# Decoder trunk, last stage of the experts: down chunks multiplied by output half, half of the result evicted ahead, read-back rows added at another place

## What is computed

```python
logits = jnp.dot(t, w_router); top_logit, top_idx = lax.top_k(logits, 2)
top_w = jax.nn.softmax(top_logit, axis=-1)
gate = jnp.einsum('tk,tke->te', top_w, jax.nn.one_hot(top_idx, 8))
for e in range(8):
    out = out + gate[:, e:e + 1] * swiglu(t, w_gate[e], w_up[e], w_down[e])   # 1024 -> 3584 -> 1024
h = h + out
u = rmsnorm(h, ple_norm_gain[i])
h = h + (p[i] @ w_ple[i]) * jax.nn.sigmoid(u @ w_ple_gate[i])
return rmsnorm(h, final_norm_gain)
```

## Time and profile before

| | us |
|---|---|
| three runs | 1537.55, 1538.18 (median), 1538.69 |
| profiled execution: its time | 1538.69 |
| its span in the trace | 1536.9 |
| what lies outside the span | 1.8 |

### The profile page before, as it was taken

How to read it: one execution, slowest core, us unless ns; L and a number is a source line. 1 busy time by engine, 2 the same in 40 slices (tenths; PEclk the granted TensorE clock), 3 DMA queues, 4 the chain that set the end, 5 groups by cost and what they waited for, 6 DMA issues and landing times.

```text
span 1536.9 us, 21230 instructions
## 1 busy us (share of the span) xinstructions
PE 1515.6 (99%) x7976; PEld 1278.5 (83%) x7976; DVE 1230.9 (80%) x1100; ACT 995.1 (65%) x852; POOL 56.7 (4%) x76
## 2 busy tenths in 40 slices
PE   7999999999999999999999999999999999999998
PEld 6988888888998888888888888888888888888876
DVE  5776545557686689888889889988988889898897
ACT  6544444346725367787786787687677787777666
POOL 5000000000000000000000000000000000010000
PEclk9999999999999999999999999999999999999999
DMA  9432765555533589999999999999999999999990
GB/s 300 142 111 84 256 207 186 186 168 182 165 113 121 172 292 363 379 376 382 379 374 384 381 370 387 373 373 389 371 376 387 372 374 393 367 381 387 372 390 30
DMA packets 206787, 453.38 MB, mean 295 GB/s; under 512 B 12488, under 2 KB 31504, under 8 KB 206480
## 3 DMA queue, kind: packets, MB, share of 16 engines
q1 hardware_dynamic: 200368, 439.22, 79.2%
q0 software_dynamic: 2880, 10.49, 1.8%
q10 hardware_dynamic: 3488, 2.99, 0.7%
HBM read 444.80 MB, written 7.86 MB: 295 GB/s over the span
## 4 chain that ended last, share of the span: by engine, by line
PE 95%; DVE 3%; ACT 1%; DMA 0%; issue 0%; SPq 0%; DVEq 0%; ACTq 0%
PE bank L1607 29%; PE bank L1609 28%; PE bank L1608 28%; PE bank L2106 2%; PE bank L1698 2%; DVE wlo L953 1%; PE bank L1805 1%; PE bank L1758 1%; PE bank L1602 1%; DMA raw<-in_w_in_dram 0%; PE bank L1772 0%; PE bank L2079 0%; PE bank L1707 0%; PE bank L1732 0%; PE bank L2088 0%; PE bank L1747 0%
## 5 line engine op out<-in xcount | busy, mean ns | idle before, releaser
L953 DVE TENSOR_TENSOR wlo<-raw,whi 128x2048 fp32r<-128x2048 f32 x415 | 936.4, 2288 | 143.1 <-ACT whi L604 91.7
L604 ACT ACTIVATE whi<-raw 128x2048 fp32r<-128x2048 f32 x341 | 636.6, 1911 | 34.3 <-DMA raw<-in_w_exp_down_dram 17.8
L1607 PE MATMUL bank<-whi,uTh 128*128 128x512 f32 (+1 forms) x1304 | 512.0, 393 | 0.9 <-DVE uTl L1019 0.5
L1609 PE MATMUL bank<-whi,uTl 128*128 128x512 f32 (+1 forms) x1304 | 503.8, 386 | 0.0
L1608 PE MATMUL bank<-wlo,uTh 128*128 128x512 f32 (+1 forms) x1304 | 502.8, 386 | 0.0
L1609 PEld LDWEIGHTS bank<-whi,uTl 128*128 128x128 f32 x1304 | 245.0, 188 | 50.7
L1607 PEld LDWEIGHTS bank<-whi,uTh 128*128 128x128 f32 x1304 | 245.2, 188 | 49.0 <-DVE uTl L1019 0.7
L1608 PEld LDWEIGHTS bank<-wlo,uTh 128*128 128x128 f32 x1304 | 245.4, 188 | 46.6
L1607 PE MATMUL bank<-whi,hTr 128*128 128x512 f32 x528 | 207.2, 392 | 0.4 <-DVE hTr L1506 0.4
L1609 PE MATMUL bank<-whi,hTr 128*128 128x512 f32 x528 | 205.7, 390 | 0.0
L1608 PE MATMUL bank<-wlo,hTr 128*128 128x512 f32 x528 | 205.5, 389 | 0.0
(11 more groups left out here) (294 smaller groups left out, 1084.1 us busy)
## 6 DMA issues: line engine op xcount, KB each, us to landing
raw<-in_w_exp_gate_dram SPq DMA_DIRECT2D x112, 1024.0 KB, 5.6
raw<-in_w_exp_up_dram SPq DMA_DIRECT2D x112, 1024.0 KB, 6.2
raw<-in_w_exp_down_dram SPq DMA_DIRECT2D x112, 1024.0 KB, 5.7
raw<-in_w_in_dram SPq DMA_DIRECT2D x28, 1024.0 KB, 5.5
raw<-in_w_ffn_gate_dram SPq DMA_DIRECT2D x11, 1024.0 KB, 5.1
raw<-in_w_ffn_up_dram SPq DMA_DIRECT2D x11, 1024.0 KB, 5.2
raw<-in_w_ffn_down_dram SPq DMA_DIRECT2D x11, 1024.0 KB, 4.9
raw<-in_w_out_dram SPq DMA_DIRECT2D x8, 1024.0 KB, 5.3
```

Source lines behind the costliest of these rows:

```text
L604: nc.scalar.activation(whi[:, s % SPLIT, :], raw[:, s % RAW, :], ACT.Copy).then_inc(hi_a, 1)
L953: return V.tensor_tensor(wlo[:, n % RAW, :], raw[:, n % RAW, :], whi[:, n % SPLIT, :].bitcast(F32), ALU.subtract).then_inc(lo_ready, 1)
L1607: T.matmul(o, sth, mvh, start=start, stop=False)
L1609: return T.matmul(o, stl, mvh, start=False, stop=stop)
```

## The change

Three edits. (1) In a down chunk PE goes over the halves outside and the rows of weights inside: banks 5, 5, 6, 6; in the last chunk of an item it counts a new semaphore `first_half` when bank 5 is finished. (2) ACT's `y_out` waits for `first_half` ahead of the first half's copy, and for the whole last chunk only ahead of the second's. (3) In the last item DVE calls `add_experts(0)` and `add_experts(1)` behind its work for chunks 38 and 39, ahead of `last_slots` and no longer behind it. The semaphores `fgp0` and `fgp1` become one that counts to two.

```diff
-        fgp = sems("fgp", DEPTH)
+        fgp = sem("fgp")
...
-                dve.wait_ge(fgp[l], 1)
+                dve.wait_ge(fgp, l + 1)
...
             def y_out(i):
-                act.wait_ge(consumed, i * EXP_LOADS + (NSTATIC + EXP_LOADS))
                 act.wait_ge(scattered, i * 16 + 16)
                 for q in range(2):
+                    if q == 0:
+                        act.wait_ge(first_half, i + 1)
+                    else:
+                        act.wait_ge(consumed, i * EXP_LOADS + (NSTATIC + EXP_LOADS))
                     nc.scalar.activation(ysb[:, q * NC:(q + 1) * NC], bank(5 + q), ACT.Copy).then_inc(y_ready, 1)
...
-            item(last_item, EXP_LOADS + 1)
+            def other_rows(n):
+
+                if LAST_UP + 1 <= n <= LAST_UP + TT:
+                    add_experts(n - LAST_UP - 1)
+
+            item(last_item, EXP_LOADS + 1, other_rows)
             last_slots()
-            add_experts(0)
-            add_experts(1)
             add_last(0)
             add_last(1)
...
-                        for c, q in [(c, q) for c in range(2) for q in range(2)]:
+                        for q, c in [(q, c) for q in range(2) for c in range(2)]:
                             cc = 2 * hf + c
                             s = slice(q * NC, (q + 1) * NC)
                             last = product(bank(5 + q), exhT[r % 2][0][:, cc, :], exhT[r % 2][1][:, cc, :], wh[:, c, s], wl[:, c, s],
                                            start=r == 0 and cc == 0, stop=end and c == 1)
+                            if end and q == 0 and c == 1:
+                                last.then_inc(first_half, 1)
```

More of the change, by code:

```diff
@@ L314, in trunk @@
         slot_ready, last_y = sem("slot_ready"), sem("last_y")
+        first_half = sem("first_half")
         consumed = sem("consumed")
@@ L1676, in forget @@
                     if c0 + n == SEQ:
-                        last.then_inc(fgp[l], 1)
+                        last.then_inc(fgp, 1)
                 def step(s):
```

## The result

The changed kernel takes 1541.22 us (median of 11 runs, 1539.47 to 1544.83); the kernel before took 1538.53 us in the same comparison (11 runs, 1536.91 to 1540.55). The ratio is 1.0019, 95% interval 1.0011 to 1.0028; the medians are 2.7 us apart, the changed kernel slower.

A forecast was written before the change was run, and what follows sets the result against it. PE was taken to bound the items and last stage, with DVE's add_last and ACT's square setting the stretch between. Banks 0, copies 0 and DVE order +1.84 us on 1538.18 gave 1540.0 us, range 1538.3 to 1541.5.

The forecast's parts named there:

- Bank order, and copies in the items: Down chunks and y_out of items 0 to 6: nothing gained or lost; bank order bounded at 1.1 us either way.
- Copies in the last item: y_out of the last item: first copy 1.36 us earlier, but DVE not free until 1498.05; alone worth about 0.2 us.
- `add_experts` ahead of `last_slots`: DVE behind chunk 42's low part: last_slots ends at 1498.13, PE's products and the end come 1.84 us later.
- the hand-over: From DVE's selectors to PE's products: PE's wait for slot_ready might cost 0.3 us more, upper bound 2.1 us.
- The rival by the clock: PE's clock falls in the 2.6 us gap before the products: about +3.1, together +4.9 us, median 1543.1; chance 0.09.
- PE's slack of 0.26 us: PE's wait ahead of tile 0's transposes, taken off the clock rival's 3.4 us of lost work.
- the likeliest case: Whole kernel: banks 0, copies 0, DVE order +1.84 us, giving a median of 1540.0 us.
- the range: Median time of the changed kernel: 1538.3 to 1541.5 us.
- its own sign of being wrong: Behind the gap ahead of the selector products: PE's clock row showing less than 1.00 would prove the prediction wrong.
- The last stage: Behind tile 0's transposes, from 1504 on: PE is full, so the end moves by the same 1.84 us.

The follow-up runs named there:

- e1: The changed kernel with the third edit undone (bank order and early copy stay): 1539.26 us for 1539.07 us of the kernel before, ratio 1.0000.
- f1: The changed kernel itself, timed and profiled again, on another chip: 1542.32 us for 1539.20 us of the kernel before, ratio 1.0017.
- g2: One more profiled execution of the unaltered changed kernel; no median given; its selector products took 3.69 us.
- e2: The kernel before with the third edit alone (old bank order, old y_out): 1541.22 us for 1539.07 us of the kernel before, ratio 1.0020.
- e3: The changed kernel with last_slots between add_experts(0) and add_experts(1): 1538.82 us for 1539.07 us of the kernel before, ratio 0.9996.
- f2: The changed kernel with 20 unread transposes on PE ahead of its wait for slot_ready: 1539.78 us for 1539.20 us of the kernel before, ratio 1.0003.
- g3: The changed kernel with 20 unread transposes ahead of PE's wait for slot_ready, timed again: 1541.06 us for 1539.17 us of the kernel before, ratio 1.0013.

## Why the prediction was right, point by point

- **Bank order, and copies in the items.** Nothing, as forecast: in `e1` both edits stand and the ratio is 1.0000. The waits that PE had in the items of the changed kernel's first profile (0.9 us from 650 to 1490) come and go: the executions `f1` and `g2` of the same kernel have none there, and `e2`, without the two edits, has 0.3.
- **Copies in the last item.** I put 0.2 us on the early copy alone. It measured 0.01 (7.85 for 7.86 us). The products did come earlier, by 0.92 us, but DVE's fourth addition was not what bound. The prediction has DVE ending last and ACT's square earlier; yet the chain of the kernel before runs from the second addition over the square, and in `e1` DVE waits 0.17 us for ACT behind all four additions. A term that was too big by its whole size, with no effect on the sum, since the third edit covered it.
- **`add_experts` ahead of `last_slots`.** Forecast +1.84 us; in the trace +1.90, and +1.88 in `e2` alone. The steps: additions from 1492.19, forecast 1492.07; selectors done at 1498.26, forecast 1498.13; both differ by the 0.1 us by which that execution was late. From the selectors' end to PE's products it took 0.24 us and not 0.06: the hand-over that no row showed, for which the upper bound had allowed 0.3. So the products came 2.04 us later and not 1.84. The transposes came only 1.90 us later, because DVE no longer waited for ACT ahead of its reciprocal: this started 0.67 us behind the start of the fourth addition (1502.90 for 1502.23) and 0.79 us before (1500.88 for 1500.09). ACT's square came 1.76 us later, counted from the last down matmul, where I had 1.3 to 1.5. `e3` shows the condition: it costs only what the selectors come later than PE.
- **The rival by the clock** had a chance of 0.09 and was taken to happen or not. It does both: 1 in 4 profiled executions, +3.1 us foretold and 3.0 measured (12.78 less 9.76), +4.9 in all foretold and 4.92 measured. That the price fits so well is in part luck. The clock was low for 6.8 us in `f1` too, 3.4 us of lost work, but 0.4 us of it were lost in the gap, where nothing ran, and PE's slack of 0.26 us, which I took off, saves nothing, since DVE's additions wait for the same products and the norm comes later with them. The rows were also misread: 1.08 us is PE's longest wait in the routing stage, not in the trace. At the kernel's start PE waits 2.87 us for DVE, and the eight transposes behind that took 1.97 us, where those at 1503.06 took 1.09; this was a hint of slower matmuls behind a wait, though with no dense work ahead of it. A fall in some executions fits the timed median (+2.7, again +3.1), which lies above the trace's 1.9, and the comparison with the filled gap, at +1.2 us, speaks for it; how often it happens is not shown. The step that failed is the one that took this as one case among others and the likeliest case as the median; a fall in some executions belongs into the forecast's own range. How many timed runs have it can't be told: a timed run gives one mean clock for the whole run, in steps of 0.001 or 1.5 us, and the falls of the routing stage (below) lower it as much as one in the gap. The rule of the Trainium skill ("TensorE: Matmul & The Clock Gate", "Why this matters for your kernels"), that idle gaps between bursts bring the clock back to its lower level, agrees with the gap of 4.2 us here. The gap of 2.8 us is shorter than those that the rule warns of, so that by its letter it did not foretell this rival; the fall came there all the same, in one execution of five.
- **The number.** The median of 1541.22 lies inside the range, 0.3 us below its upper edge and 1.2 above the likeliest case: 0.35 us because the kernel before measured 1538.53 and not 1538.18, 0.06 us by the trace, and 0.8 us that the trace of the profiled execution doesn't show. `f1`, the same kernel once more, has 1542.32, outside it (the kernel before was 0.7 us higher in that set, too). And its own sign of being wrong, a clock below 1.00 behind the gap, is there in one execution of four. The mechanism was right; that the median stayed in the range owes something to luck.
- **The last stage** takes up nothing, as forecast: PE is busy in 25.00 of 25.00 us behind the transposes.

## What to carry to other kernels

Work that is moved ahead on one engine pushes something back on the same engine: look at what stands between the old and the new place, and who waits for it. Here there was no gap to fill, only three short operations that another engine waited for; the right move was to take those out of the full stretch, to any place behind their inputs where the engine has time. A result that is ready earlier (the copy here) is worth what the last of its partners allows, so find the partner before speeding up the first. And a wait of PE can cost more than its length: filling it with transposes that nobody needs gave back most of the surplus where the wait itself could not be removed. It is no sure cure: the kernel fills the waits of its routing stage with such transposes already, and the clock falls there in every profiled execution.

## What the runs showed of the hardware

PE's clock behind a gap is not a property of the kernel alone. With 2.8 us of idle PE behind 840 us of dense matmuls the same program kept 1.00 in three profiled executions and went to 0.50 in one; with 4.2 us it went to 0.50 in the one execution that was profiled, and in none of the three profiled ones with the gap filled. The longer gap was not the dearer one: the fall cost 3.0 us behind 2.8 us of gap and 1.7 us behind 4.2. In the first the clock was down before the products began (0.50 over 1497.5 to 1498), in the second it fell about 1 us after they had begun (0.70 over 1502 to 1504).

The clock also falls in the routing stage, in all 14 profiled executions here (0.50 to 0.63 over 532 to 536), although PE is busy there and the kernel already puts filling transposes into its waits. From PE's transposes at about 525 us to those of the second item's tokens at about 650 it took 126.1 us in one execution and 122.8 in another. The first of the two is `f2`, with these stretches in it (clock 0.83, 0.50, 0.52):

```profile
525.00:532.00 7.00, 5.19 (x35) 4.79 (x34) 4.79 (x20) 2.26 (x2) 0.53 (x1) 0.83 0.90 297
532.00:536.00 4.00, 4.00 (x22) 4.00 (x21) 1.53 (x10) 1.35 (x3) 0.10 (x1) 0.50 0.05 16
536.00:540.00 4.00, 4.00 (x21) 4.00 (x20) 0.72 (x6) 0.00 (x0) 0.00 (x0) 0.52 0.00 0
```

The second is `g2`, the changed kernel (clock 1.00, 0.57, 1.00):

```profile
525.00:532.00 7.00, 5.41 (x45) 4.94 (x46) 5.11 (x26) 2.21 (x4) 0.65 (x2) 1.00 0.81 272
532.00:536.00 4.00, 4.00 (x23) 4.00 (x23) 1.37 (x9) 0.73 (x2) 0.00 (x0) 0.57 0.01 3
536.00:540.00 4.00, 3.91 (x36) 3.67 (x34) 1.39 (x3) 1.19 (x2) 0.00 (x0) 1.00 0.00 0
```

At 0.50 the first spends (0.17 x 7 + 0.50 x 4 + 0.48 x 4) / 0.5 = 10.2 us, the second 0.43 x 4 / 0.5 = 3.4 us. The difference of 6.8 us at half speed is 3.4 us of work, and the two are 3.3 us apart. So this stage alone sets executions 3.3 us apart, and the runs above 1542 us that stayed in `f2` and `g3` need no new cause, though no timed run shows its own place of loss. A whole execution's span can't be compared to better than 3 us here, while distances counted from a matmul inside the stretch repeat to 0.03 us.
